# Down product of the experts in three products of split operands instead of f32, in a fused mixture-of-experts decoder trunk on one core

## The reference

```
def moe_ffn(x, ...):
    scores = sigmoid(xt @ router_w)                 # 64 experts, the 8 best of each token
    ...
    def expert_block(args):                         # up to 128 rows of one expert
        tok, e = args
        xb = xt[tok]
        h = silu(xb @ w_gate[e]) * (xb @ w_up[e])   # 1024 -> 256
        return h @ w_down[e]                        # 256 -> 1024
    y = lax.map(expert_block, ...) * row_gate       # and summed by token
```

## Time and profile before

| | us |
|---|---|
| median of three runs | 2527.16 (2517.16 to 2552.97) |
| the profiled execution | 2509.57 |
| its span in the trace | 2507.9 |
| TensorE busy | 2308.0 (92%), 9437 matmuls and transposes |
| VectorE busy | 1607.2 (64%) |
| ScalarE busy | 1076.4 (43%) |
| GpSimd busy | 842.1 (34%) |
| loads and stores issued by SyncE | 517.92 MB, 55.4% of 16 engines |
| gathers and scatters issued by GpSimd | 73.91 MB, 12.5% of 16 engines |

### The profile page before, as it was taken

The page is one execution under the profiler, slowest core; times in us unless marked ns, Lnnn a source line. Parts: engine busy times, 40 slices in busy tenths (PEclk is TensorE's granted clock), DMA queues, the critical chain, the costliest instruction groups (busy, mean ns, idle before and its releaser), DMA issues.

```text
span 2507.9 us, 32871 instructions
## 1 busy us (share of the span) xinstructions
PE 2308.0 (92%) x9437; PEld 1629.8 (65%) x9437; DVE 1607.2 (64%) x1737; ACT 1076.4 (43%) x1215; POOL 842.1 (34%) x698
## 2 busy tenths in 40 slices
PE   7948889999999999869999999797999999999994
PEld 4413566766666766559988888455666666776663
DVE  4874557776666666452377887436676676677665
ACT  3651135555555555322243333112555555555552
POOL 4960215554444444200000000002454454454431
PEclk9968889999999999979999999898999999999997
DMA  6210359999999999633322223033999999999994
GB/s 214 67 34 0 126 199 357 371 371 367 361 335 355 368 353 356 187 132 93 93 75 68 85 84 101 28 118 126 326 362 360 349 354 359 361 377 358 344 346 131
DMA packets 197117, 592.57 MB, mean 236 GB/s; under 512 B 26605, under 2 KB 96277, under 8 KB 161732
## 3 DMA queue, kind: packets, MB, share of 16 engines
q1 hardware_dynamic: 165140, 517.92, 55.4%
q0 software_dynamic: 31920, 73.91, 12.5%
HBM read 579.16 MB, written 51.38 MB: 251 GB/s over the span
## 4 chain that ended last, share of the span: by engine, by line
PE 63%; DMA 17%; DVE 6%; issue 4%; POOL 2%; ACT 1%; POOLq 1%; DVEq 0%; ACTq 0%
PE PS L1355 17%; PE PS L1376 13%; PE PS L1464 10%; DMA BIG<-xrows,IDXG 9%; DMA acc<-BIG,IDXS 7%; PE PS L1448 5%; PE PS L1246 5%; PE PS L1342 4%; PE PS L1280 2%; POOL IDXG L571 1%; PE PS L1477 1%; PE PS L1502 1%; DVE BIG L1016 1%; PE PS L1326 1%; PE PS L1364 1%
## 5 line engine op out<-in xcount | busy, mean ns | idle before, releaser
L998 DVE TENSOR_TENSOR WL<-W,WH 128x2048 fp32r<-128x2048 f32 x276 | 621.5, 2294 | 197.4 <-ACT WH L679 185.9
L679 ACT ACTIVATE WH<-W 128x2048 fp32r<-128x2048 f32 x276 | 512.2, 1906 | 42.3 <-DVE IDX L976 42.3
L1376 PE MATMUL PS<-W,BIG 128*128 128x512 f32 x1104 | 501.0, 597 | 2.0 <-DVE BIG L1010 2.0
L1355 PE MATMUL PS<-WH,XH 128*128 128x512 f32 x1104 | 446.6, 405 | 8.8 <-DVE XL L991 8.8
L1355 PE MATMUL PS<-WH,XL 128*128 128x512 f32 x1104 | 434.7, 394 | 0.0
L1355 PE MATMUL PS<-WL,XH 128*128 128x512 f32 x1104 | 432.6, 392 | 0.0
L589 POOL DMA_INDIRECT acc<-BIG,IDXS x138 | 223.9, 1622 | 508.6 <-issue 489.1
L1376 PEld LDWEIGHTS PS<-W,BIG 128*128 128x128 f32 x1104 | 200.9, 192 | 203.3 <-issue 200.7
L574 POOL DMA_INDIRECT BIG<-xrows,IDXG x138 | 273.6, 1983 | 119.5 <-POOL IDXG L571 119.5
L571 POOL COPY IDXG<-IDX 128x1 uint32 (+1 forms) x138 | 217.8, 1578 | 74.4 <-PE PS L1342 37.9
L1355 PEld LDWEIGHTS PS<-WH,XH 128*128 128x128 f32 x1104 | 209.5, 190 | 48.3 <-DVE XL L991 9.6
(11 more groups left out here) (233 smaller groups left out, 3058.9 us busy)
## 6 DMA issues: line engine op xcount, KB each, us to landing
W<-in_exp_w_gate SPq DMA_DIRECT2D x138, 1024.0 KB, 7.5
W<-in_exp_w_up SPq DMA_DIRECT2D x138, 1024.0 KB, 8.8
W<-in_exp_w_down SPq DMA_DIRECT2D x138, 1024.0 KB, 9.0
RAW<-in_w_kv SPq DMA_DIRECT2D x48, 512.0 KB, 3.8
RAW<-in_attn_w_q SPq DMA_DIRECT2D x24, 512.0 KB, 3.7
W<-in_conv_w_in SPq DMA_DIRECT2D x8, 1024.0 KB, 11.4
acc<-BIG SPq DMA_DIRECT2D x9, 512.0 KB, 3.7
W<-in_conv_w_out SPq DMA_DIRECT2D x4, 1024.0 KB, 6.6
```

Source lines behind the costliest of these rows:

```text
L679: A(WH[:, s, c, :], W[:, 3 - 3 * s + c, :], ACT.Copy).then_inc(s_wh[l], 1)
L998: v.tensor_tensor(WL[s][:, c, :], W[:, 3 - 3 * s + c, :], WH[:, s, c, :].bitcast(F32), ALU.subtract).then_inc(s_wl[l], 1)
L1355: last = mm(PS[:, 3 + s, :].rearrange("p (a b) -> p a b", a=2), a, w, start=(k == 0 and i == 0), stop=(k == KT - 1 and i == 2))
L1376: last = mm(PS[:, 5 + h, :], HTm[:, s, k * P:(k + 1) * P], wd[:, k, h * 512:(h + 1) * 512], start=(k == 0), stop=(k == 1))
```

## The change

The down product takes split operands like the gate and up products. ScalarE writes the high part of the down weights (`down_high`, at the end of its step, for block b + 1, ahead of the output copies) and of the transposed hidden rows (`hidden_high`, at the start of its step); VectorE writes the low parts (`down_low` at the end of its step, over the weights in their slot; `hidden_low` at the start). TensorE runs 12 matmuls for 8. ScalarE copies both halves of the output, VectorE none. The new buffers lie in gaps of the layout; one of them is where the shared experts' tiles were, so ScalarE waits for their store before its first step. Two pairs of semaphores become one each, as there are not enough of them. The counts waited for are adapted, since `s_wh` and `s_wl` now rise by three in a step.

```diff
@@ layout
+        _, WDH1, HTL, _, HTH, WDH0, _, WDL = lay_out([("to_WDH1", [8192 + 10240], F32), ("WDH1", [2, D], F32R), ("HTL", [2, F], F32R),
+                                                      ("to_HTH", [20736 - 12800], F32), ("HTH", [2, F], F32R),
+                                                      ("WDH0", [2, D], F32R), ("to_WDL", [256], F32),
+                                                      ("WDL", [SLOTS, CH], F32R)])
+        WDH = (WDH0, WDH1)
@@ SyncE, load_gate_up
-                        sp.wait_ge(s_wl[l], b * 2 - 3 + c)
+                        sp.wait_ge(s_wl[l], 1 + c if isinstance(b, int) and b == 2 else b * 3 - 6 + c)
@@ GpSimd, scatter
-                    pool.wait_ge(s_ya[l], b + 1)
-                    pool.wait_ge(s_yv[l], b + 1)
+                    pool.wait_ge(s_ya[l], b * 2 + 2)
@@ ScalarE
+                def down_high(b, s, it):
+                    act.wait_ge(s_mw[l][5 - 3 * s], it * 16 + 16)
+                    if not (isinstance(b, int) and b < 2):
+                        act.wait_ge(s_yd[l], b - 1)
+                    A(WDH[s].rearrange("p k n -> p (k n)"), W[:, 5 - 3 * s, :], ACT.Copy).then_inc(s_wh[l], 1)
+
+                def hidden_high(b, s):
+                    act.wait_ge(s_ht[l], b + 1)
+                    if not (isinstance(b, int) and b < 2):
+                        act.wait_ge(s_yd[l], b - 1)
+                    A(HTH[:, s, :], PS[:, 2, 0:F], ACT.Copy).then_inc(s_hh[l], 1)
...
-                def out_low(b, s):
+                def out(b, s):
...
-                    A(YB[:, s, 0:512], PS[:, 5, :], ACT.Copy).then_inc(s_ya[l], 1)
+                    for h in range(2):
+                        A(YB[:, s, h * 512:(h + 1) * 512], PS[:, 5 + h, :], ACT.Copy).then_inc(s_ya[l], 1)
 
                 def step(b, s, it, more):
+                    hidden_high(b, s)
                     if more:
                         weights_high(b + 2, s, it + 1)
                     if more or s == 0:
                         silu(b + 1, 1 - s)
                     if more:
                         rows_high(b + 2, s)
-                    out_low(b, s)
+                    if more or s == 0:
+                        down_high(b + 1, 1 - s, it + s)
+                    out(b, s)
...
+                down_high(0, 0, 0)
+                for k in range(2):
+                    act.wait_ge(s_acc[l][k], 16 * NT // 2)
@@ VectorE
+                def down_low(b, s, copies):
+                    dve.wait_ge(s_wh[l], copies)
+                    v.tensor_tensor(WDL[:, 5 - 3 * s, :], W[:, 5 - 3 * s, :],
+                                    WDH[s].rearrange("p k n -> p (k n)").bitcast(F32), ALU.subtract).then_inc(s_wl[l], 1)
+
+                def hidden_low(b, s):
+                    dve.wait_ge(s_hh[l], b + 1)
+                    v.tensor_tensor(HTL[:, s, :], PS[:, 2, 0:F], HTH[:, s, :].bitcast(F32), ALU.subtract).then_inc(s_he[l], 1)
 
                 def step(b, s, more):
-                    hidden_T(b, s)
+                    hidden_low(b, s)
                     if more:
                         weights_low(b + 2, s)
                     if more or s == 0:
                         hidden(b + 1, 1 - s)
                     if more:
                         rows_low(b + 2, s)
-                    out_high(b, s)
+                    if more or s == 0:
+                        down_low(b + 1, 1 - s, b * 3 + 8 if more else n * 6)
@@ TensorE
-                def down_proj(b, s, it):
+                def down_proj(b, s, splits):
                     pe.wait_ge(s_he[l], b + 1)
-                    pe.wait_ge(s_mw[l][5 - 3 * s], it * 16 + 16)
+                    pe.wait_ge(s_wl[l], splits)
                     if not (isinstance(b, int) and b == 0):
-                        pe.wait_ge(s_ya[l], b)
-                        pe.wait_ge(s_yv[l], b)
-                    wd = W[:, 5 - 3 * s, :].rearrange("p (k n) -> p k n", k=2)
+                        pe.wait_ge(s_ya[l], b * 2)
+                    wdl = WDL[:, 5 - 3 * s, :].rearrange("p (k n) -> p k n", k=2)
                     for h in range(2):
+                        cols = slice(h * 512, (h + 1) * 512)
                         for k in range(2):
-                            last = mm(PS[:, 5 + h, :], HTm[:, s, k * P:(k + 1) * P], wd[:, k, h * 512:(h + 1) * 512],
-                                      start=(k == 0), stop=(k == 1))
+                            hh, hl = HTH[:, s, k * P:(k + 1) * P], HTL[:, s, k * P:(k + 1) * P]
+                            wh, wl = WDH[s][:, k, cols], wdl[:, k, cols]
+                            for i, (a, w) in enumerate(((hh, wh), (hh, wl), (hl, wh))):
+                                last = mm(PS[:, 5 + h, :], a, w, start=(k == 0 and i == 0), stop=(k == 1 and i == 2))
                     last.then_inc(s_yd[l], 1)
```

More of the change, by code:

```diff
@@ L215, in build @@
         s_ob = sem("overflow_bases")
-        s_pj = [sem(f"onehots{i}") for i in range(2)]
-        s_tb = [sem(f"table_steps{i}") for i in range(2)]
+        s_pj = sem("onehots")
+        s_tb = sem("table_steps")
         s_tab = sem("tables_ready")
@@ L240, in build @@
         s_ht = [sem(f"hidden_transposed{i}") for i in range(2)]
-        s_he = [sem(f"hidden_T_copied{i}") for i in range(2)]
+        s_hh = [sem(f"hidden_T_high{i}") for i in range(2)]
+        s_he = [sem(f"hidden_T_low{i}") for i in range(2)]
         s_yd = [sem(f"expert_out{i}") for i in range(2)]
-        s_ya = [sem(f"expert_out_low_copied{i}") for i in range(2)]
-        s_yv = [sem(f"expert_out_high_copied{i}") for i in range(2)]
+        s_ya = [sem(f"expert_out_copied{i}") for i in range(2)]
         s_scat = [sem(f"scattered{i}") for i in range(2)]
@@ L721, in moe @@
                     step(it * 2 + 1, 1, it, True)
-                step(n * 2 - 2, 0, None, False)
-                step(n * 2 - 1, 1, None, False)
+                step(n * 2 - 2, 0, n - 1, False)
+                step(n * 2 - 1, 1, n - 1, False)
             act.wait_ge(s_vps, 1)
@@ L996, in weights_low @@
                     for c in range(2):
-                        dve.wait_ge(s_wh[l], b * 2 + 1 + c)
+                        dve.wait_ge(s_wh[l], b * 2 + 1 + c if isinstance(b, int) and b < 2 else b * 3 + c)
                         v.tensor_tensor(WL[s][:, c, :], W[:, 3 - 3 * s + c, :], WH[:, s, c, :].bitcast(F32),
@@ L1037, in moe @@
                 rows_low(1, 1)
+                down_low(0, 0, 5)
                 step(0, 0, True)
@@ L1327, in moe @@
                                   start=(n == 0 and j == 0), stop=(n == NT - 1 and j == 7))
-                    last.then_inc(s_tb[l], 1)
+                    last.then_inc(s_tb, 1)
                 sh_gate_up(3)
@@ L1347, in gate_up @@
                     pe.wait_ge(s_xl[l], b + 1)
-                    pe.wait_ge(s_wl[l], b * 2 + 2)
+                    pe.wait_ge(s_wl[l], b * 2 + 2 if isinstance(b, int) and b < 2 else b * 3 + 1)
                     if not (isinstance(b, int) and b < 2):
@@ L1385, in step @@
                         rows_T(b + 2, s, it + 1)
-                    down_proj(b, s, it)
+                    down_proj(b, s, b * 3 + 5 if more or s == 0 else n * 6)
                 rows_T(0, 0, 0)
```

17 lines of the change are left out of this document (4 added, 13 removed).

## The result

The changed kernel took 2591.66 us (median of four runs, 2588.73 to 2598.42) against 2540.06 for the kernel before in the same session: a ratio of 1.0256, 95% interval 1.0207 to 1.0305. The forecast was 2541 with a range up to 2590, so the result lies just outside it, on the slower side.

A forecast was written before the change was run, and what follows sets the result against it. TensorE was taken to set the step at 10.02 us, gather round trip and DMA engines close behind. Steps of 10.1 (136 x 0.08 = +11), fluctuations +5, ends -2 gave +14 profiled, 2541 us as a median, range 2480 to 2590.

The forecast's parts named there:

- TensorE: Down product: 12 split matmuls take 2.74 us instead of 3.44, saving 0.70 a step if TensorE sets it (9.32).
- ScalarE, VectorE: Their work in the expert loop: 7.9 and 8.7 us a step, both fitting in TensorE's 9.32.
- The gather: Gather issued 6.42 us after the output copies' start instead of 5.62; its round trip sets 9.85 us a step.
- The down weights, earlier: ScalarE wants the down weights 7.6 us after the down product's end; a late load delays output copies, scatter and gather.
- L: Landing time of the down weights' load, taken as 8.7 us; L + 21.6 spans three steps, 10.1 a step.
- the scatter's ring: On GpSimd, each scatter issued within 1.2 us of the previous one's landing, so lateness carries on; the forecast gave no term.
- Rival 3: ScalarE's copy waits for late down weights: slower by over 2%, 2602 us as a median at L = 10; chance 0.20.
- The DMA engines: Transfers in the expert loop need 9.6 us a step whatever TensorE does; their busy share stays at 0.98.
- The 44 us of waits (heavy scatters, first steps) stay: Loop time beyond TensorE's own 1363 us of work, taken as unchanged by the change.
- The signs: Marks of a right forecast, among them TensorE idling 0.6 to 0.9 us a step for the gather, busy share falling.
- rival 2: GpSimd's index copy slips ahead of VectorE's pair in a near tie: faster by about 2%, 2468 us; chance 0.10.
- Rival 4: Only the arithmetic counts and TensorE's 9.32 us step rules: 136 x -0.70 = -95, 2430 us as a median; chance 0.02.

The follow-up runs named there:

- e10: Changed kernel without the down weights' low part, output copies ahead of ScalarE's down-weight copy, half of each down load left out: 1.0025 of the time before.
- e13: Changed kernel without the low part of the down weights and with half of each down load left out: 0.9895 of the time before.
- e2: Changed kernel without the low part of the down weights (VectorE subtracts 16 columns only): 1.0179 of the time before.
- e1: Changed kernel with the scatter's index copy moved ahead of the gather on GpSimd: 1.0241 of the time before.
- e7: Kernel before with 6 of its 8 down matmuls and none of the change's other work: 0.9896 of the time before.
- e4: Kernel before with one idle 128x2048 subtraction, both inputs in SBUF, ahead of VectorE's output copy: 1.0439 of the time before.
- e6: Kernel before with one idle 128x2048 subtraction, one input from PSUM, ahead of VectorE's output copy: 1.0401 of the time before.
- e8: Kernel before with VectorE's pair of weight subtractions waiting for GpSimd's index copies for the gather: 0.9888 of the time before, 2501.38 us.

## Why the prediction was wrong, point by point

- *TensorE*: right. The 12 down matmuls take 2.77 us in e10's chain (2.74 forecast); in the changed kernel they start 0.23 apart.
- *ScalarE, VectorE*: right as to their work, which fits into the step. VectorE's sum asked whether 8.7 fits in 9.32, though; it did not ask beside which of GpSimd's instructions the new 2.25 would lie. Measured per step in the loops: 8.1 and 8.65 (1103.6 and 1176.2 / 136).
- *The gather*: the number was right to 0.03 us, in the step shown, for a kernel in which nothing holds the scatter (e13). In the changed kernel the gather is queued behind the scatter on GpSimd and goes out 8.58 after the output copies.
- *The down weights, earlier*: L was forecast at 8.7, and in the step shown it is 8.8 (718.38 less 709.60). The mechanism is real (e2), but not the first: it comes out once the scatter's ring has been taken away, and then L is 10.3 where it rules, so the forecast's step of 10.1 would have been too short without the scatter as well (10.5). The parts of its L + 21.6 add up to L + 21.5, which changes no conclusion. Rival 3 gave 2602, close to the 2591.66 measured, by luck: its place was ScalarE, and there the waits are 32 us in the profile that is 88.6 us longer in the loops.
- *The DMA engines*: they don't set the longer step. Their share fell from 0.98 to 0.94 and 0.95, where "DMA stays at its share" was forecast.
- *TensorE's clock*: "so nothing comes from it" was wrong. It is granted to 0.96 and 0.98 in the loops, for 1.00 and 0.99 before, and was in no term of the sum.
- *Ends*: right; all of the 88.8 us is in the loops but for 0.2.
- **The step that failed** is in the sum: "The 44 us of waits (heavy scatters, first steps) stay", and with it "136 x 0.08 = +11". Against these the loops of the profiles show +88.6, 11.00 a step for 10.35, with the scatter at 22% of the chain instead of 7% and 114 scatters held instead of 23. I had the scatter's ring in the earlier trace rows and gave it no term: only the gather had a round trip. I also had the index copy's two durations in the earlier trace rows and used them for the gather only. The scatter's own copy comes to lie beside the new subtraction, and the output copies end later on one engine than before on two; by that reading either would move the scatter's issue towards the pair, where the kernel before shows 3.06 us for it in the heavy stretch. How the loss is shared between them, the late load and the clock stays open; the copy alone isn't it (e1).
- *The signs* did not separate the stories. TensorE does wait for the gather, 0.97 us a step (134.2 / 138) for 0.6 to 0.9 forecast, and its busy share fell from 92% to 87%, but the gather is late because it stands behind the scatter.
- *The tie* (rival 2) did not matter: index copies for the gather take 1.38 us in the mean, over 1 as forecast.
- *Rival 4* fell with the result, and e7 shows why: about the same saving of TensorE, with none of the change's other work, is worth 1%.

The Trainium skill, "SBUF — State Buffer", section "Who interferes with whom", has VectorE and GpSimd share ports under an exclusive lock. e4 against e6 agrees for the index copy (0.92 with both inputs in SBUF, 0.22 with one in PSUM). The slow issue of the scatter looks like the same wait: index copies made beside such a subtraction end 0.04 us after it in the median, and scatters issued beside it 1.34 after, close to the 1.44 that one takes alone. A subtraction that starts after the scatter's issue does not lengthen it (at most 1.62).

## What to carry to other kernels

Look for every round trip that hides just behind the busiest engine, not only for the one that the change touches, and put each queue's new instruction beside what the other engines do at that moment: work that fits into an engine's idle time can still hold a neighbour. Test it with an idle instruction of the same size in the old kernel (e4): one run showed what a late scatter costs, which the sum of durations could not. And where a short DMA issue races with a long run of another engine, try a wait that lets it go first; here that is worth 1.1%, as much as the saved matmuls are by themselves, and e8 is the version to keep.

## What was not expected of the hardware

- A GpSimd copy of 128 indices takes 0.18 us alone, and 0.92 in the mean of e4 (2.20 in one step of the changed kernel) beside a subtraction whose inputs both lie in SBUF; with one input in PSUM it takes 0.22 (e6).
- Issuing a scatter takes GpSimd 1.4 to 1.6 us, but 3.3 in the step shown: when it starts while a subtraction with both inputs in SBUF runs, it ends some 1.34 us after that subtraction. Started just ahead of the subtraction it is not held.
- A late scatter keeps the next one late. The kernel before gets into this and out again within one execution, and in e8's session its runs spread over 47 us (2508.04 to 2555.29) where those of e8 spread over 8; that the one explains the other fits, but is not shown.
